# Two-layer hybrid diffusion step: second gate in its own bank, last pair by output half, side loads later, prompt columns first

## The reference, cut to what matters

```python
mod = silu(cond) @ w_mod[l] + b_mod[l]          # six vectors of 1024 per stream
h = rmsnorm(x, g1) * (1 + sc1) + sh1
z = h @ w_in                                     # u_a, q_b, k_b, v_b, q_c, kv_c, kr_c, three gates
ya = pooling(u_a); yb = windowed_attention(q_b, k_b, v_b, cache); yc = latent_attention(q_c, kv_c, kr_c, cache)
merged = sum(sigmoid(gate_i) * (y_i @ w_br_i) for i in (a, b, c))
x = x + g1_mod * (merged @ w_out)
h = rmsnorm(x, g2) * (1 + sc2) + sh2
aff = softmax(h @ w_router); vals, idx = top_k(aff, 2 * tokens // 16)     # each of 16 experts chooses its tokens
o = (silu(h[idx] @ w_gate) * (h[idx] @ w_up)) @ w_down * vals
x = x + g2_mod * scatter_add(o, idx)
```

## Time and profile before

| | before |
|---|---|
| time, median of 3 runs | 1796.28 us (1795.14 to 1796.75) |
| the profiled execution's own time | 1796.94 us |
| its span, first to last instruction | 1794.8 us |
| TensorE busy | 1700.1 us (95%), mean granted clock 0.997 |
| VectorE, ScalarE, POOL busy | 649.4, 289.6, 118.6 us |
| moved by DMA | 533.80 MB, 297 GB/s over the span |

### The profile page before, as it was taken

One profiled execution on the slowest core, in us unless ns is written; L12 is line 12 of the kernel. 1 busy time (PEld: TensorE's weight loads), 2 busy tenths in 40 slices (PEclk: granted clock), 3 DMA queues, 4 the chain that ended last, 5 costly groups with the idle time before them and its releaser, 6 DMA issues.

```text
span 1794.8 us, 18804 instructions
## 1 busy us (share of the span) xinstructions
PE 1700.1 (95%) x7152; PEld 802.0 (45%) x7152; DVE 649.4 (36%) x1379; ACT 289.6 (16%) x735; POOL 118.6 (7%) x161
## 2 busy tenths in 40 slices
PE   6999999999999988898999999999999999988988
PEld 2465566654434332242345555666553432423322
DVE  1356555567222110121124566555661211201211
ACT  2234222111200010000022432220021100100100
POOL 1151000000000000000012500000000000000000
PEclk9999999999999999999999999999999999999999
DMA  9430333655999999999993212337559999999997
GB/s 377 190 124 24 117 118 129 269 202 202 406 428 428 429 428 427 431 427 427 427 365 121 100 52 113 118 129 296 231 209 410 428 428 428 429 428 428 429 427 317
DMA packets 49105, 533.80 MB, mean 297 GB/s; under 512 B 5840, under 2 KB 6896, under 8 KB 10384
## 3 DMA queue, kind: packets, MB, share of 16 engines
q1 hardware_dynamic: 45776, 524.39, 71.0%
q0 software_dynamic: 2112, 7.97, 1.2%
q10 hardware_dynamic: 1152, 0.56, 0.1%
HBM read 530.76 MB, written 2.13 MB: 297 GB/s over the span
## 4 chain that ended last, share of the span: by engine, by line
PE 73%; DMA 23%; DVE 3%; issue 1%; ACT 0%; SPq 0%; POOL 0%; DVEq 0%
PE bank L1995 21%; DMA ring<-in_w_moe 21%; PE bank L1605 12%; PE bank L1624 7%; PE bank L1670 6%; PE bank L2032 5%; PE bank L1852 5%; PE bank L1706 2%; DMA ring<-in_w_mix 2%; PE bank L1766 2%; PE bank L1919 1%; PE bank L1633 1%; PE bank L1741 1%; PE bank L1596 1%; PE bank L1593 1%; PE bank L1790 1%
## 5 line engine op out<-in xcount | busy, mean ns | idle before, releaser
L1605 PE MATMUL bank<-hT,ring 128*128 128x384 f32 x768 | 260.0, 492 | 5.2 <-DVE xn L1076 5.1
L1995 PE MATMUL bank<-M,hT 128*64 128x512 f32 x992 | 221.4, 595 | 17.2 <-DMA M<-in_w_moe 16.1
L1995 PE MATMUL bank<-ring,hT 128*64 128x512 f32 x1024 | 227.1, 595 | 10.0 <-DMA ring<-in_w_moe 10.0
L1605 PEld LDWEIGHTS bank<-hT,ring 128*128 128x128 f32 x768 | 144.5, 191 | 108.9 <-issue 8.2
L1995 PEld LDWEIGHTS bank<-ring,hT 128*64 128x64 f32 x1024 | 72.5, 137 | 156.1 <-issue 139.5
L1995 PEld LDWEIGHTS bank<-M,hT 128*64 128x64 f32 x992 | 70.0, 137 | 158.6 <-issue 134.5
L1624 PE MATMUL bank<-M,ring 128*128 128x384 f32 x384 | 138.0, 504 | 0.7 <-ACT M L772 0.7
L1995 PE MATMUL bank<-ring,M 128*64 128x512 f32 x512 | 115.4, 596 | 18.0 <-DMA ring<-in_w_moe 18.0
L1995 PE MATMUL bank<-M 128*64 128x512 f32 x512 | 116.0, 596 | 14.2 <-DMA M<-in_w_moe 14.2
L1670 PE MATMUL bank<-ring,hT 128*128 128x512 f32 (+1 forms) x288 | 117.4, 568 | 3.8 <-DVE hT L1068 2.1
L968 ACT ACTIVATE hT<-bank 128x512 f32<-128x512 f32 x32 | 19.1, 597 | 570.2 <-PE bank L1995 570.2
(11 more groups left out here) (238 smaller groups left out, 1539.1 us busy)
## 6 DMA issues: line engine op xcount, KB each, us to landing
ring<-in_w_moe SPq DMA_DIRECT2D x96, 2048.0 KB, 30.7
M<-in_w_moe SPq DMA_DIRECT2D x94, 2048.0 KB, 30.4
ring<-in_w_mix SPq DMA_DIRECT2D x110, 1024.0 KB, 5.0
arena<-in_w_moe SPq DMA_DIRECT2D x2, 2048.0 KB, 14.6
ring<-in_w_mix SPq DMA_DIRECT2D x4, 576.0 KB, 4.9
arena<-in_bias_rows POOLq DMA_DIRECT2D x4, 512.0 KB, 6.2
g2slot<-in_bias_rows POOLq DMA_DIRECT2D x4, 512.0 KB, 6.9
M<-in_counts POOLq DMA_DIRECT2D x2, 768.0 KB, 12.9
```

Of the source, the lines that this page charges most:

```text
L1605: ins = mm(ps[:, 0:TOK], w[:, q, (j % 4) * P:(j % 4 + 1) * P], hT[:, 4 * h + q, :], start=(h == 0 and q == 0), stop=(h == 1 and q == 3))
L1995: ins = mm(bank[b][64 * e:64 * e + 64, :], lhs(e, 4 * h + q), w[:, q, :], start=(h == 0 and q == 0), stop=(h == 1 and q == 3))
```

## The change

Seven edits:

- `plan_banks`: the result of gate (0, 1) goes to bank 6 in place of 7.
- Tables: the identity and `pair` (130 columns) come first; SP loads them ahead of x, and the other 1168 columns behind the first unit that refills a slot (index 9), with a semaphore `tables_in` of their own.
- POOL issues the rows as before, with a semaphore `rows_in`, then waits until index 12 has landed, in both layers, and issues the other seven loads.
- The first four feature blocks: `h_front` takes the prompt columns of both blocks first, then the sample columns, and TensorE's first products of segment 0 wait for the prompt columns alone. `mod_cols` makes `1 + sc` in one operation with the addition.
- Layer 1: VectorE copies modulation row 0 behind the first normalised tile.
- Last pair of a layer: down (0,0), (0,1), combine 0, (1,0), (1,1), combine 1, and the doubles in that order.
- A tensor `lead` of 58 columns before `M` moves `M`, and all that is allocated behind it, by 256 bytes.

```diff
-NLOAD = 8
+LEAD = 58
+NLOAD = 7
...
-_sizes = [("ident", P), ("ones", P), ("slots0", P), ("slots1", P), ("pair", 2), ("fold", NE),
+_sizes = [("ident", P), ("pair", 2), ("ones", P), ("slots0", P), ("slots1", P), ("fold", NE),
...
+NFIRST = P + 2
...
+        if m == 0:
+            use(("gate", 0, 1), 6)
         use(("o", m), 6)
         for j in (2 * m, 2 * m + 1):
-            use(("gate", j // 8, j % 8), 7)
+            if j != 1:
+                use(("gate", j // 8, j % 8), 7)
             use(("br", j // 8, j % 8), 7)
...
         ring = sb("ring", [P, RING, UNIT])
+        sb("lead", [P, LEAD])
         M = sb("M", [P, 20160])
...
-            sp.dma_start(const[:, :], a["const"]).then_inc(const_in, 16)
+            sp.dma_start(const[:, 0:NFIRST], a["const"][:, 0:NFIRST]).then_inc(const_in, 16)
...
                     sp.dma_start(ring[:, s, 0:width], a["w_mix"][l, n, :, 0:width]).then_inc(landed[s], 16)
+                    if l == 0 and n == ISSUE[RING]:
+                        sp.dma_start(const[:, NFIRST:NCONST], a["const"][:, NFIRST:NCONST]).then_inc(tables_in, 16)
...
                 if l == 0:
                     pool.wait_ge(landed[slot_of(UNITS[5])], 16)
+                pool.dma_start(rows[:, :], a["rows"][l].partition_broadcast(P)).then_inc(rows_in, 16)
+                pool.wait_ge(*unit_landing(l, ("seg", 2, 0)))
                 for dst, src in loads:
                     pool.dma_start(dst, src).then_inc(layer_in, 16)
...
-            def h_evac(l, name, kb):
-                k = 0
-                ps = wait_full(dve, l, (name, kb))
-                step(V.tensor_scalar(hT[:, kb, 0:P], ps[:, 0:P], amp[k][:, kb, 0:1], shift[k][:, kb, 0:1], ALU.mult, ALU.add))
-                read(l, (name, kb), V.tensor_scalar(hT[:, kb, P:TOK], ps[:, P:TOK], amp[k][:, kb, 1:2], shift[k][:, kb, 1:2],
-                                                    ALU.mult, ALU.add))
+            def h_front(l):
+                for kb in FRONT[0::2]:
+                    ps = wait_full(dve, l, ("h1", kb))
+                    V.tensor_scalar(hT[:, kb, 0:P], ps[:, 0:P], amp[0][:, kb, 0:1], shift[0][:, kb, 0:1], ALU.mult, ALU.add)\
+                        .then_inc(front_dve, 1)
+                dve.wait_ge(front_dve, 2 * (l + 1))
+                for kb in FRONT[0::2]:
+                    ps = bank[turn(l, ("h1", kb))[0]]
+                    read(l, ("h1", kb), V.tensor_scalar(hT[:, kb, P:TOK], ps[:, P:TOK], amp[0][:, kb, 1:2],
+                                                        shift[0][:, kb, 1:2], ALU.mult, ALU.add))
...
-                if l > 0:
-                    mod_row(l, 0)
                 first_variance(0)
                 first_variance(1)
                 normalise(0)
+                if l > 0:
+                    mod_row(l, 0)
...
-                dve.wait_ge(layer_in, 16 * NLOAD * (l + 1))
+                dve.wait_ge(tables_in, 16)
+                dve.wait_ge(rows_in, 16 * (l + 1))
                 step(V.tensor_scalar(negsink[:, :], rows[:, ROW_SINK:NROW], -1.0, None, ALU.mult))
...
+                    if last:
+                        begin_pair(BANK_T, 2)
+                        project_down(0, 1)
+                        combine(0)
+                        project_down(1, 0)
+                        project_down(1, 1)
+                        combine(1)
+                        return
```

More of the change, by code:

```diff
@@ L386, in hybrid_step @@
         const_in = sem("const_in")
+        tables_in = sem("tables_in")
+        rows_in = sem("rows_in")
+        front_act = sem("front_act")
+        front_dve = sem("front_dve")
         layer_in = sem("layer_in")
@@ L519, in _, with wait_pair @@
             sp.dma_start(x[:, 1:3, :], a["x_sample"][0].rearrange("(t p) d -> p t d", p=P)).then_inc(x_in, 16)
-            def wait_pair(l, gr, c, j):
-                g, h = (j // 2, j % 2) if j < 8 else (4 + j % 2, j // 2 - 4)
+            def wait_pair(l, gr, c, j, last=False):
+                g, h = (j // 2, j % 2) if j < 8 or last else (4 + j % 2, j // 2 - 4)
                 if h == 0:
@@ L621, in _ @@
                 loads = [
-                    (rows[:, :], a["rows"][l].partition_broadcast(P)),
                     (poolw, a["pool_w"][l].rearrange("g c d -> c g d")),
@@ L733, in mod_row @@
                 read(l, ("mod", i), F(row_of(i), ps[:, :], ACT.Copy))
-            def h_evac(l, name, kb):
-                k = 0
-                ps = wait_full(act, l, (name, kb))
-                step(F(hT[:, kb, 0:P], ps[:, 0:P], ACT.Identity, scale=amp[k][:, kb, 0:1], bias=shift[k][:, kb, 0:1]))
-                read(l, (name, kb), F(hT[:, kb, P:TOK], ps[:, P:TOK], ACT.Identity, scale=amp[k][:, kb, 1:2],
-                                      bias=shift[k][:, kb, 1:2]))
+            def h_front(l):
+                for kb in FRONT[1::2]:
+                    ps = wait_full(act, l, ("h1", kb))
+                    F(hT[:, kb, 0:P], ps[:, 0:P], ACT.Identity, scale=amp[0][:, kb, 0:1], bias=shift[0][:, kb, 0:1])\
+                        .then_inc(front_act, 1)
+                act.wait_ge(front_act, 2 * (l + 1))
+                for kb in FRONT[1::2]:
+                    ps = bank[turn(l, ("h1", kb))[0]]
+                    read(l, ("h1", kb), F(hT[:, kb, P:TOK], ps[:, P:TOK], ACT.Identity, scale=amp[0][:, kb, 1:2],
+                                          bias=shift[0][:, kb, 1:2]))
             def h_raw(l, kb):
@@ L781, in _ @@
                 act.wait_ge(cols_ready, 2 * l + 1)
-                for kb in FRONT[1::2]:
-                    h_evac(l, "h1", kb)
+                h_front(l)
                 if l > 0:
@@ L799, in _ @@
                     F(qctok[:, t, 0:256], ps[:, 256:512], ACT.Copy).then_inc(cseg_read, 1)
+                act.wait_ge(rows_in, 16 * (l + 1))
                 act.wait_ge(layer_in, 16 * NLOAD * (l + 1))
@@ L1135, in _ @@
                 mod_cols(l, 0, 0, 0, KB // 2, 1)
-                for kb in FRONT[0::2]:
-                    h_evac(l, "h1", kb)
+                h_front(l)
                 if l > 0:
@@ L1664, in segment @@
                         for q in range(4):
-                            if s == 0 and t == 0:
-                                if h == 0:
-                                    wait_read(pe, l, ("h1", q))
-                                elif q == 0:
-                                    pe.wait_ge(back_ready, 8 * (l + 1))
+                            if s == 0 and h == 0 and t == 0:
+                                pe.wait_ge(front_act if q % 2 else front_dve, 2 * l + q // 2 + 1)
+                            if s == 0 and h == 0 and t == 1:
+                                wait_read(pe, l, ("h1", q))
+                            if s == 0 and h == 1 and t == 0 and q == 0:
+                                pe.wait_ge(back_ready, 8 * (l + 1))
                             ins = mm(ps[:, 0:n], hT[:, 4 * h + q, t * P:(t + 1) * P], w[:, q, 0:n],
@@ L1983, in project @@
                             begin_pair(b, PROJECT[b])
-                        j = 12 * c + (2 * g + h if g < 4 else 4 + 2 * h + g)
+                        j = 12 * c + (2 * g + h if g < 4 or last else 4 + 2 * h + g)
                         s = DOUBLES[j % ND]
@@ L2048, in pair_step @@
                     project_down(0, 1)
-                    if last:
-                        combine(0)
                     project_down(1, 1)
-                    if not last:
-                        combine(0)
+                    combine(0)
                     combine(1)
@@ L2101, in expert_units @@
     out = out.reshape(L, NP, 12, P, 2 * UNIT)
-    return np.concatenate([out[:, :, 0:8], out[:, :, 8:12:2], out[:, :, 9:12:2]], axis=2)
+    out[:, :NP - 1, 8:12] = out[:, :NP - 1][:, :, [8, 10, 9, 11]]
+    return out
 def kernel(**inputs):
```

9 lines of the change are left out of this document (4 added, 5 removed).

## The result

| | before | changed |
|---|---|---|
| median | 1795.71 us (1793.36 to 1796.75, 4 runs) | 1782.53 us (1778.52 to 1783.28, 4 runs) |
| ratio | 1 | 0.9917, 95% interval 0.9904 to 0.9931 |
| profiled execution | 1796.94 us, span 1794.8, clock 0.997 | 1778.52 us, span 1776.4, clock 1.000 |
| TensorE busy | 1700.1 us | 1694.8 us |

The median is the predicted 1782.6. So the number needs a look behind it: where the 18.4 us came from, and why the median shows only 13.2.

The account below looks back on a forecast made before the run. TensorE was taken to bound the mixing stages and the weight stream the experts', in turns. Gains summed to 13.7 us, taken from the three-run median of 1796.28: 1782.6 us, range 1777 to 1788.

Parts of the forecast that it names:

- The frame: Mixing is TensorE's time, experts the stream's at 428 GB/s; time saved in mixing moves the end one for one.
- the stream does not move: Rival: experts' stream sets the end and hides mixing time; only the last tail's 1.1 us is left, 1795.2; chance 0.05.
- both of the shifted slots: Two rivals: M's moved slots load faster (1778.0, chance 0.08) or slower (at 5%, 1805.6, chance 0.05).
- The start of layer 0: Up to segment 1: fewer table bytes ahead (1.8 us) and prompt columns first (0.57) make TensorE 3.8 us earlier.
- The lower bound of 1.9: Start of layer 0: the gain is only 1.9 us where the tables move at half the pace.
- the lower end of 1790.6: Whole kernel: the time in us with the lower bounds of all terms, said not to fall together.
- The rival of the small DMA: Start: a small load costs as much as a large one, saving 0.9 us, not 1.8; time 1783.5; chance 0.10.
- The estimate by the Trainium skill's figure: Start: at 0.95 us for 64 KB, the first table part gives back 0.75 us; time 1783.4.
- Gates and tails: Gate (0,1) loses its 2.55 us bank wait in each layer; each layer's reordered last pair ends 1.1 us earlier.
- I take 1.6 because nothing else stood before this one: Layer 1, second gate: without its wait the clock fall behind it goes too, 1.6 us, between 0 and 1.6.
- The sum of 13.7: Whole kernel: all forecast gains in us together, 3.8 + 2.55 + 1.1 + 1.0 + 2.55 + 1.6 + 1.1.

Follow-up runs that it names:

- experiment 10: The changed kernel without the tensor `lead`, so M and what lies behind it at the old addresses: 1780.74 us.
- experiment 11: The kernel of experiment 6 with the first four feature blocks scaled whole, TensorE waiting for whole blocks: 1778.35 us.
- Experiment 7: The kernel of experiment 6 with gate (0,1) in bank 7 again: 1784.48 us.
- experiment 8: The changed kernel without POOL's wait for segment 2, so all side loads are issued at once: 1787.78 us.
- experiment 6: The changed kernel with only column(6), the column products of head pair 2, moved behind its branch: 1777.18 us.
- experiment 5: The changed kernel with all column products of the summed modulation rows moved behind the branch: 1777.92 us.

## Why the prediction came out right

**The frame.** Time saved in a mixing stage moved the end one for one: what was gained by 460 us was still there at 860 but for 0.2 us, and the streams ran at 428 GB/s as before. The rival "the stream does not move" is dead, and so are both of the shifted slots (experiment 10).

**The start of layer 0**, 3.8 forecast, 3.97 measured. The first matmul moved by 1.88 us (1.8 forecast). 0.27 of it was lost on the way to segment 0; the prompt columns gave their 0.57 (0.58 in experiment 11); segment 1 did not wait at all (the forecast let the unit land 0.3 us behind TensorE; in three other traces of the new start it waited 0.16 to 0.34). The 0.27 went into the first turns of x. Before and after:

```profile
17.37 1.53 PE L1577 MATMUL bank<-const,xn 128*128 128x128 f32 x12
```

```profile
15.60 2.57 PE L1599 MATMUL bank<-const,xn 128*128 128x128 f32 x12
```

Their longer time first uses up the old wait for a unit (0.68 us at 20.57) and then delays what follows. From the first matmul to the column step it is 8.36 us before and 8.63 here; in the nine traces where these turns took up to 2.25 us it is 8.35 to 8.37, experiment 10 with the same start among them, and in the four where they took more it is 8.49 to 8.63. So this is a matter of the single execution and not of the change. What makes the turns slower was not tried.

The lower bound of 1.9 for this start, with the tables at half the pace, is not what its own sum gives: 0.60 MB at 195 GB/s take 1.5 us more than forecast, which leaves 2.3. Nothing but the lower end of 1790.6 rests on it.

The rival of the small DMA falls: the 65 KB landed 2.0 us after issue, the columns 2.2 in place of 5.0. DMA issues of the changed kernel, 0 to 60 us (KB, us to landing):

```profile
arena<-in_ctx_kr POOLq DMA_DIRECT2D x1, 16.0 KB, 7.1
...
const<-in_const SPq DMA_DIRECT2D x1, 65.0 KB, 2.0
...
cols<-in_cols SPq DMA_DIRECT2D x1, 68.0 KB, 2.2
```

The estimate by the Trainium skill's figure (DMA: Bandwidth & Descriptors, section "Bandwidth") would have taken 0.75 us of this saving away; the table there is for loads that GpSimd issues, and this one is SP's. The trace shows none of it lost: the first matmul moved by the 1.8 of the sum, and x's sample tiles landed 6.1 us after their issue, 8.0 before. Why the small load cost no more is not shown; the DMA engines were not full meanwhile, with 130 GB/s at 3 to 4 us where before had 322. The moved side loads cost nothing, as forecast, and landed quicker, 7.1 us for 15.1.

**Gates and tails, each a little too small.** 2.55 was 2.8 to 2.9, and 1.1 was 1.45. Most of both misses has one cause: I took an idle time, or a sum of durations, where the distance between starts was wanted. A branch that lasts 2.85 us by its row lets the next matmul start 2.69 later (152.43 to 155.12), a half that lasts 3.65 is followed at 3.48 (1762.15 to 1765.63); the ends are modelled and overlap the next start. With durations of 3.65 and 3.03 the sum for the tail came to 15.6 us where the starts show 15.37. The Trainium skill says it (Perfetto Trace Analysis, section "Tensor Engine Instruction (MATMUL, LD_WEIGHTS)"): the end of a matmul in the profile is an estimate and not an observation; these rows agree, the modelled ends lie 0.16 and 0.17 us behind the next start. Another 0.1 us of the gate's miss lies behind its start: from its start to the turns it takes 5.26 us behind the wait (161.81 to 167.07) and 5.16 without one (155.12 to 160.28).

**The clock, right in sum and wrong in its step.** The step "I take 1.6 because nothing else stood before this one" gave the fall in layer 1 to the gate, and left the two behind column(6) as they were. Experiment 7 bears out the first half: with the gate's wait back as the only long one in the attention, falls come back, on average one a run. The second half failed: the falls behind column(6) come in some runs only. In nine traces with that wait the branch behind it slowed five times in layer 0 and seven in layer 1, the four runs of the result had none, two, three and three by their spans (1776.4 to 1781.1, 1.65 us each), and the profiled one happened to be the first.

So the hit of 0.1 us on 1782.6 is partly luck. Over eight runs the changed kernel's mean is 1781.5, over forty the kernel before's is 1796.7: 15.3 us, 13.4 of it the parts and some 1.9, one fall a run, the clock. The sum of 13.7 was 1.6 short: 0.5 in the gates, 0.5 in the tails, 0.3 in the clock, the rest in small pieces. What hid it is mostly the four runs of before beside the result, whose mean of 1795.4 is 1.4 below that of all forty; the changed kernel's four lie 0.2 above the mean of its eight.

## What to carry to other kernels

Look for a wait of TensorE in dense work even where it lasts 0.7 us: it can cost 1.7 more by the clock, and it makes the runs scatter. Moving one instruction group behind the next (experiment 6) was worth 2.4 to 4.4 us, about as much as the new order of the last pairs (2.9). And work out a path from start to start, never from modelled ends.

## What the runs showed of the hardware

- Thirteen traces have 19 falls from 2.4 to 1.2 GHz ahead of their last product, of some 1.6 to 1.7 us lost each where it could be read. All stood in mixing stages and began within 3.1 us of the end of a wait of TensorE; none stood in the experts' stages, although TensorE waits there too (1.24 us in the earlier trace rows).
- Whether a wait brings one is not told by its length alone. 2.55 us at the second gate brought none in layer 0 in four traces and one in layer 1 in all four; 0.67 at column(6) brought twelve in eighteen; 0.68 at 447 us none at all in thirteen; at segment 1, 1.23 and 1.72 none, 2.58 and 3.44 one each; 1.02 at 19 us, in experiment 8, one. What else decides was not tried.
- Three kernels without the waits at the second gate and at column(6) repeat within 0.08 us (experiment 6, four runs), 0.6 (experiment 5, five runs) and 0.8 (experiment 11, four runs). With the wait at column(6) the changed kernel scatters over 4.8 us in eight runs and the kernel before, with both, over 8.1 in forty.
